# The softmax normalisation of the attention probabilities, on GpSimd instead of VectorE

## What is computed

```python
h = rmsnorm(x, g_pre_mix)
q, k, v, u, g = split_projection(h, w_in)          # one combined projection
# attention: windows of 128 keys back plus own chunk, 16 heads, 2 KV heads
s = einsum(q, k) * scale + bias                     # bias also holds the mask
m = max(max(s), sink)
p = exp(s - m)
denom = sum(p) + exp(sink - m)
o = einsum(p / denom, v)
# convolution branch: depthwise, 31 taps, over the same frames
y = silu(layernorm(depthwise_conv(u, w_dw) + b_dw)) @ w_conv_out
x = x + rmsnorm((g0 * o + g1 * y) @ w_out)
x = x + rmsnorm((silu(h2 @ w_gate) * (h2 @ w_up)) @ w_down)     # h2 = rmsnorm(x)
```

## Time and profile before

| what | us |
|---|---|
| median of three runs | 4013.1 |
| the runs | 3986.5 to 4016.0 |
| the profiled execution: its time | 4013.1 |
| the profiled execution: its span | 4011.3 |

### The profile page before, as it was taken

How to read it: one execution, slowest core, us unless ns; L and a number is a source line. 1 busy time by engine, 2 the same in 40 slices (tenths; PEclk the granted TensorE clock), 3 DMA queues, 4 the chain that set the end, 5 groups by cost and what they waited for, 6 DMA issues and landing times.

```text
span 4011.3 us, 42778 instructions
## 1 busy us (share of the span) xinstructions
PE 3457.1 (86%) x17022; PEld 2884.5 (72%) x17022; DVE 1997.4 (50%) x2932; ACT 1244.9 (31%) x1986; POOL 1436.3 (36%) x710
## 2 busy tenths in 40 slices
PE   2378987999998888999979988999978978969997
PEld 2257756887776756887757756887878876869986
DVE  1296963005599952005696952005595963130033
ACT  1013452224323442224213442224212433122222
POOL 1153233444442233444452233444453202233333
PEclk8689998999998998999989998999988976679999
DMA  1212112233321122223311122223311110212221
GB/s 58 83 63 69 48 54 89 95 96 109 116 81 52 48 80 68 95 95 110 111 63 53 53 79 69 95 95 106 103 58 62 45 32 32 72 48 90 90 79 59
DMA packets 88166, 300.94 MB, mean 75 GB/s; under 512 B 10337, under 2 KB 17585, under 8 KB 87329
## 3 DMA queue, kind: packets, MB, share of 16 engines
q1 hardware_dynamic: 87968, 298.21, 22.5%
HBM read 289.22 MB, written 12.17 MB: 75 GB/s over the span
## 4 chain that ended last, share of the span: by engine, by line
PE 57%; DVE 29%; issue 6%; POOL 4%; ACT 3%; DMA 1%; SPq 0%; DVEq 0%; ACTq 0%; POOLq 0%
PE PS L564 36%; DVE y L1039 15%; PE PS L600 5%; PE PS L602 5%; PE PS L601 5%; DVE p L1123 3%; POOL w_lo L465 3%; DVE p L1102 2%; DVE pt_lo L1114 2%; PE PS L678 1%; PE PS L684 1%; DVE PS L1080 1%; PE PS L581 1%; DVE x L1085 1%; DVE xs L1050 1%
## 5 line engine op out<-in xcount | busy, mean ns | idle before, releaser
L465 POOL TENSOR_TENSOR w_lo<-w_raw,w_hi 128x1024 fp32r<-128x1024 f32 x496 | 1326.3, 2675 | 2379.3 <-ACT w_hi L779 2378.3
L564 PE MATMUL PS<-h_hi,w_hi 128*128 128x512 f32 (+1 forms) x3352 | 1095.9, 360 | 240.5 <-POOL w_lo L465 186.5
L779 ACT ACTIVATE w_hi<-w_raw 128x1024 fp32r<-128x1024 f32 x496 | 525.2, 1059 | 2088.8 <-PE PS L564 1513.8
L564 PE MATMUL PS<-h_hi,w_lo 128*128 128x512 f32 (+1 forms) x3352 | 1089.3, 358 | 0.0
L564 PE MATMUL PS<-h_lo,w_hi 128*128 128x512 f32 (+1 forms) x3352 | 1081.6, 356 | 0.0
L1039 DVE SCALAR_TENSOR_TENSOR y<-u,dw,y 128x512 f32<-128x512 f32 (+1 forms) x960 | 854.2, 954 | 0.0
L564 PEld LDWEIGHTS PS<-h_hi,w_hi 128*128 128x128 f32 x3352 | 606.8, 194 | 333.8 <-POOL w_lo L465 184.8
L564 PEld LDWEIGHTS PS<-h_lo,w_hi 128*128 128x128 f32 x3352 | 606.0, 194 | 91.1
L564 PEld LDWEIGHTS PS<-h_hi,w_lo 128*128 128x128 f32 x3352 | 605.1, 194 | 85.6
L1288 DVE TENSOR_TENSOR f<-PS,tmp 128x512 f32<-128x512 f32 (+1 forms) x88 | 61.6, 700 | 889.0 <-PE PS L564 866.5
L1294 DVE TENSOR_TENSOR f_lo<-f,f_hi 128x1024 fp32r<-128x1024 f32 (+1 forms) x88 | 209.2, 2378 | 249.3 <-ACT f_hi L993 249.3
(11 more groups left out here) (166 smaller groups left out, 3837.4 us busy)
## 6 DMA issues: line engine op xcount, KB each, us to landing
w_raw<-in_w_stream SPq DMA_DIRECT2D x496, 512.0 KB, 3.4
xs<-in_x_prompt SPq DMA_DIRECT2D x16, 512.0 KB, 3.7
x<-in_x_prompt SPq DMA_DIRECT2D x4, 2048.0 KB, 8.6
out_y_prompt<-x SPq DMA_DIRECT2D x4, 2048.0 KB, 7.2
gp<-in_g_post SPq DMA_DIRECT2D x4, 1024.0 KB, 4.8
toep_dram<-toep_dram SPq DMA_DIRECT2D x1, 3048.0 KB
bias<-toep_dram SPq DMA_DIRECT2D x1, 2048.0 KB, 8.6
bias<-toep_dram SPq DMA_DIRECT2D x2, 1024.0 KB, 6.0
```

Source lines behind the costliest of these rows:

```text
L465: nc.gpsimd.tensor_tensor(w_lo[:, g % 2, :], w_raw[:, g % RAW, :], w_hi[:, g % 2, :].bitcast(F32), ALU.subtract).then_inc(w_lo_ok, 1)
L564: last = nc.tensor.matmul(PS[:, k0 + off, 0:n], w, x[:, k, c0:c0 + n], start=first and k == 0, stop=stop and k == KT - 1)
L779: A(w_hi[:, g % 2, :], w_raw[:, g % RAW, :], ACT.Copy).then_inc(w_hi_ok, 1)
```

## The change

The four `tensor_scalar` on VectorE, and the wait ahead of them, are taken out of `denominator`. GpSimd gets in each gate step, after its `split_lo`, one `tensor_tensor` multiply of the whole tile `p` (128x4x256, in place) with `rl`, which is read broadcast over the 256 columns of each head. It waits for `rl_ok` and gives `p_ok`. In the last block's sixteenth gate step GpSimd does it for units 15 to 19.

```diff
@@ in the GpSimd program
                     split_lo(split_step(b, s))
+                    if S_A <= s < S_C:
+                        i = s - S_A
+                        for n in [i] if i < 15 else range(i, units(b)):
+                            pool.wait_ge(rl_ok, U0[b] + n + 1)
+                            nc.gpsimd.tensor_tensor(p[:], p[:], rl.unsqueeze(2).broadcast_to([P, 4, 2 * P]),
+                                                    ALU.mult).then_inc(p_ok, 1)
                     if s == S_C:
@@ in the VectorE program, denominator(b, n)
                 link(TT(lsum, lsum, es, ALU.add))
                 nc.vector.reciprocal(rl, lsum).then_inc(rl_ok, 1)
-                dve.wait_ge(rl_ok, gu + 1)
-                for h in range(4):
-                    ins = nc.vector.tensor_scalar(p[:, h, :], p[:, h, :], rl[:, h:h + 1], None, ALU.mult)
-                ins.then_inc(p_ok, 1)
```

## The result

Over 16 runs the changed kernel takes 4048.9 us in the median and the kernel before, over 16 runs, 4002.2. The ratio is 1.0109, 95% interval 1.0076 to 1.0144: slower, by 44 us, with the interval from 30 to 58. The forecast was 62 us slower and 4075 us, with a range of 4035 to 4125. So the sign and the place were right, and the size was too large: 62 us forecast, 44 measured. The profiled execution of the changed kernel has a span of 4055.0 us, 43.7 over that of the profiled execution before.

What follows compares the result with a forecast made beforehand. VectorE was taken to bound the gate steps. Per unit, minus 1.17 us of relief plus a 2.11 us stop gave +0.94; 64 units plus the last block's 1.2 us made 62 us on 4013.1, so 4075 us, range 4035 to 4125.

Steps and rivals of the forecast that it cites:

- the sign and the place: The change makes the program slower, by 62 us, nearly all of it in the units inside the gate steps.
- VectorE sets the pace in the gate steps: Gate steps, 10.97 us a unit: VectorE's gains or losses are the program's until TensorE, about 1 us behind, becomes late.
- The relief is 1.17 us a unit: On VectorE: four scalings of 1.06 us and 0.11 us of waiting for the reciprocal go away.
- GpSimd's operation stops VectorE, on top of `w_lo`'s stop: Gate-step units: the multiply stops a VectorE operation for 2.11 us, and `w_lo`'s stop is still paid in full.
- I take 2.38: GpSimd's added multiply in each unit: priced at 2.38 us, like `w_lo`, with a stop of 2.11 us.
- The bounds, 1.29 and 3.6: GpSimd's multiply: 1.29 us if the repeated operand reads free, 3.6 us, one and a half times `w_lo`, if slower.
- Counting: Sum over the program: 64 gate-step units times 0.94 us, 60.2 us, plus 1.2 us for the last block's units.
- The sixteenth units' +1.0: Unit 15, where only two taps follow: its transposes wait for `p` until about 3.1 us after, +1.0 us.
- The last units: Units 16 to 19 of the last block: three of four later multiplies hide behind scores, the last costs +1.2 us.
- The Trainium skill's rule on the shared ports: VectorE and GpSimd's exclusive port lock, held the whole instruction: by its letter a 2.38 us stop, 79 us in sum.
- TensorE's side: Gate steps: later probabilities covered by 2.7 us; TensorE, 9.99 us a unit against 11.9, waits longer at no cost.
- that rival: TensorE's clock gives way in the gate steps: at a mean of 0.7, 2.9 us a unit lost, 4197 us; chance 6%.

Runs made afterwards that it cites:

- The relief alone: Kernel before with the normalisation left out altogether, TensorE's transposes waiting for the reciprocal instead: 3936.1 us, ratio 0.9837.
- the waiting `w_lo`: Kernel before with `w_lo` in the gate steps held until VectorE's last tap of the step is issued: 3912.7 us, ratio 0.9792.
- the added gap: Kernel before with VectorE waiting, ahead of the gate steps, after four of seven taps for GpSimd's `w_lo` of the next step: 3956.5 us, ratio 0.9907.

## Why the prediction was right, and where its size was off

*VectorE sets the pace in the gate steps.* Right. The relief alone is worth 59 us, and a second multiply adds its whole stop to the unit, 1.64 us.

*The relief is 1.17 us a unit.* Right: 1.09 without the normalisation. In odd units 0.11 of it is not had, since `query_lo` waits for `qs_hi` just then (start 1291.11, 0.02 after the reciprocal's end).

*GpSimd's operation stops VectorE, on top of `w_lo`'s stop.* Right. The taps are stopped by both, one after the other, for 3.75 us.

*"I take 2.38, since the instruction has two inputs in SBUF and 1024 results like `w_lo`".* This is the term that was mis-sized. The operation takes 1.90 us and stops VectorE for 1.64 (1.62 where it is alone). The net price of a unit is then 1.64 less 1.17, or 0.47 us, where the prediction had 0.94; measured between the traces, 0.49. The bounds, 1.29 and 3.6, held it; no row showed a repeated operand, and I priced it as a full-width one. With a full-width operand the price is the forecast one, and so is the time.

*Counting.* 60 intervals by 0.49 are 29.7 us; with the last block's four more, 31.3 us of gate steps. The sixteenth units' +1.0, which I had counted, falls behind them, where some 7 us appear: 0.9 a block are this chain, and for the rest I had nothing. The median's 47 us and the ratio's 44 are 6 to 9 us above these two; the interval from 30 to 58 us covers it, and where they lie stays open. With the right price of the multiply my sum would have come to some 31 us. The measured 44 lie above that by what I lacked, and that this brings them nearer to my 62 is luck.

*The last units.* I had 1.2 us there, for a multiply of 2.38 in the open. The very last transposes start 2.21 us after their reciprocal in both traces of the changed kernel, and 1.48 after it in both before: 0.7 us. The last block's gate steps as a whole grew by 7.8 us in the first pair of traces and by 10.2 in the second.

*The Trainium skill's rule on the shared ports* (page "SBUF — State Buffer", section "SBUF: two separate sides"). By its letter, a hold for the whole instruction, the stop of the multiply would be 1.89 us; it is 1.64, as `w_lo`'s is 2.11 of 2.38. The direction and the kind of operation agree, the length is 0.25 us less in both.

*TensorE's side.* Its clock did not fall (1.00 in the stretch), and that rival is gone. The later probabilities are covered, as I had it: VectorE is busy 99% of the stretch. TensorE's waits for `p` did not grow, against what I had said (7.5 us in the stretch, from 8.8). That nothing waits for the later `w_lo` held too, but it belongs to the next step, not to the one after next. And I read TensorE's room wrongly. I took its busy time in the trace of before, 9.99 us a unit, for a floor; with the clock at 1.00 and nothing to wait for it does a unit in 9.55. The clock is not the whole of this: in the changed kernel it is at 1.00 as well, and TensorE, which waits within the stretch, still shows 10.04 us busy a unit (150.62 by 15). The forecasts for the scaling on ScalarE, for the waiting `w_lo` and for both (10.0 to 10.5 us) were too high for this reason.

```profile
PE PS L654 <- POOL p L510: 7.5, 8, 2.4
```

## What to carry to other kernels

Before work is moved to GpSimd, look at what VectorE runs beside it. If its operands all lie in SBUF, a `tensor_tensor` on GpSimd costs VectorE nearly GpSimd's whole duration, here 1.64 us paid for 1.17 saved. Put the work on ScalarE, or let GpSimd run beside VectorE's PSUM reads: one wait on a counter that was already there was worth 2% of this kernel. Work that is put ahead of another copy on ScalarE also moves what depends on that copy; here the move was itself a part of the gain.

Price an operation with a broadcast operand by a row of its own kind, or by a bound to both sides; by a full-width operation on the same engine it came out 0.5 us of 2.4 too dear. And an engine's busy time is no floor while its clock is below full speed or it waits within the stretch.

## What the runs showed of the hardware that I had not expected

- GpSimd can be held off for many VectorE operations, not for one. In each of the twelve traces without the added gap at least one `w_lo` of 2.4 us lasted 19.7 to 25.0 us, where VectorE ran 27 and more taps without a pause, and each of these ended at the `tensor_scalar` behind them; with the gap, the longest in the kernel before was 7.5 us. It costs the program about 20 us each time that it falls badly. That it makes most of the spread of the kernel before (3962 to 4027 us over 16 runs) is likely, since with the gap five runs lie within 11 us, but only one of those 16 has a trace to show it.
- A `tensor_scalar` on GpSimd, 128x256, takes 0.93 us and stops a tap beside it for 0.24 in the unit shown; the `tensor_tensor` of 128x1024 takes 1.90 or 2.38 and stops it for 1.64 or 2.11.
- A broadcast second operand makes GpSimd's `tensor_tensor` 20% shorter: 1.90 for 2.36 us, 1024 elements a row.
